# Gates and gelu rebuilt from exponentials, two projection panels swapped, in a one-core transformer kernel

## What is computed

```
lg_f = jax.nn.log_sigmoid(decay_f.astype(f32))
ret = (jax.nn.silu(rg.astype(f32)) * ret).astype(h.dtype)
```

```
h = jax.nn.gelu(blocks @ w1[j] + b1[j])
gate = jax.nn.sigmoid(gate_logits.astype(jnp.float32)).reshape(B, S, G, HPG, NSA_N_BRANCH)
```

## Time and profile before

| | us |
|---|---|
| median of 3 runs | 2376.28 |
| lowest, highest | 2376.14, 2379.73 |
| the profiled execution's own time | 2385.43 |
| its span in the profile | 2384.1 |
| ACT_TABLE_LOAD, each | 1.283 |

### The profile page before, as it was taken

One profiled execution on the slowest core, in us unless ns is written; L12 is line 12 of the kernel. 1 busy time (PEld: TensorE's weight loads), 2 busy tenths in 40 slices (PEclk: granted clock), 3 DMA queues, 4 the chain that ended last, 5 costly groups with the idle time before them and its releaser, 6 DMA issues.

```text
span 2384.1 us, 28303 instructions
## 1 busy us (share of the span) xinstructions
PE 2247.6 (94%) x11771; PEld 1653.6 (69%) x11771; DVE 1029.0 (43%) x1878; ACT 712.0 (30%) x1233; POOL 96.4 (4%) x100
## 2 busy tenths in 40 slices
PE   7999799888989989899989999999999999999998
PEld 6866588773433333378766788888878777888887
DVE  5337464441322323343557554243442455433335
ACT  4324344410100000132456333123133462331330
POOL 2100001001000000000000000000000000000001
PEclk9989899988999999999989999999999999999999
DMA  5232232268999999742110233232142201332320
GB/s 196 92 122 80 93 134 96 73 232 340 427 426 428 426 427 427 334 139 73 36 71 1 89 106 103 92 100 95 53 155 81 79 2 54 107 106 89 106 89 35
DMA packets 106740, 370.26 MB, mean 155 GB/s; under 512 B 15169, under 2 KB 20673, under 8 KB 94321
## 3 DMA queue, kind: packets, MB, share of 16 engines
q1 hardware_dynamic: 103584, 361.58, 40.1%
q0 software_dynamic: 3024, 6.83, 0.9%
HBM read 368.32 MB, written 4.19 MB: 156 GB/s over the span
## 4 chain that ended last, share of the span: by engine, by line
PE 81%; DMA 10%; DVE 5%; ACT 2%; issue 1%; POOL 0%; SPq 0%; DVEq 0%; ACTq 0%; POOLq 0%
PE PB L455 55%; PE PB L1909 9%; PE PB L472 5%; PE PB L774 4%; PE PB L465 3%; DMA Z<-in_w_exp_gate 3%; PE PB L666 3%; DMA FH_raw<-in_w_exp_gate 1%; DMA FL_raw<-in_w_exp_gate 1%; DMA Z<-in_w_exp_down 1%; DMA W_raw<-in_w_exp_down 1%; PE PB L790 1%; DMA FL_raw<-in_w_exp_down 1%; PE PB L671 1%; DVE W L447 1%
## 5 line engine op out<-in xcount | busy, mean ns | idle before, releaser
L455 PE MATMUL PB<-W,FH 128*128 128x512 f32 (+1 forms) x1792 | 556.0, 392 | 10.6 <-DVE FL L835 6.7
L447 DVE TENSOR_TENSOR W<-R,W 128x2048 fp32r<-128x2048 f32 (+1 forms) x128 | 291.3, 2276 | 609.6 <-ACT W L439 609.6
L439 ACT ACTIVATE W<-R 128x2048 fp32r<-128x2048 f32 (+1 forms) x128 | 243.4, 1902 | 646.8 <-PE PB L455 639.7
L455 PEld LDWEIGHTS PB<-W,FH 128*128 128x128 f32 x1792 | 330.9, 189 | 79.5 <-DVE FL L835 8.0
L455 PE MATMUL PB<-W,hid 128*128 128x512 f32 x1536 | 349.4, 389 | 0.0
L455 PE MATMUL PB<-W,FL 128*128 128x512 f32 (+1 forms) x896 | 347.8, 388 | 0.0
L455 PE MATMUL PB<-FH,W 128*128 128x512 f32 (+1 forms) x1152 | 325.7, 367 | 4.5 <-DVE FL L560 4.5
L455 PEld LDWEIGHTS PB<-W,hid 128*128 128x128 f32 x1536 | 288.1, 188 | 59.8
L455 PEld LDWEIGHTS PB<-FH,W 128*128 128x128 f32 x1152 | 209.6, 190 | 40.6 <-issue 5.0
L455 PE MATMUL PB<-FL,W 128*128 128x512 f32 (+1 forms) x576 | 211.2, 367 | 0.0
L455 PEld LDWEIGHTS PB<-W,FL 128*128 128x128 f32 x896 | 169.1, 189 | 34.7
(11 more groups left out here) (335 smaller groups left out, 2587.5 us busy)
## 6 DMA issues: line engine op xcount, KB each, us to landing
R<-in_mlp_w_up SPq DMA_DIRECT2D x32, 1024.0 KB, 5.2
R<-in_mlp_w_down SPq DMA_DIRECT2D x32, 1024.0 KB, 4.9
Z<-in_w_exp_down SPq DMA_DIRECT2D x14, 2048.0 KB, 29.4
Z<-in_w_exp_up SPq DMA_DIRECT2D x13, 2048.0 KB, 35.2
R<-in_w_exp_gate SPq DMA_DIRECT2D x11, 2048.0 KB, 32.3
W_raw<-in_w_exp_up SPq DMA_DIRECT2D x10, 2048.0 KB, 31.6
R<-in_w_exp_up SPq DMA_DIRECT2D x9, 2048.0 KB, 30.8
R<-in_w_in SPq DMA_DIRECT2D x12, 1024.0 KB, 5.4
```

The costliest lines, as they stand in the source:

```text
L439: k.A.e.activation(w.splits[w.split_of[u]][0][:, 0:m], w.rows(u), ACT.Copy).then_inc(*w.hi.tick(u))
L447: k.V.e.tensor_tensor(wl[:, 0:m], w.rows(u), wh[:, 0:m].bitcast(F32), ALU.subtract).then_inc(*w.lo.tick(u))
L455: ins = te.matmul(bank, l, r, start=(start and n == 0), stop=(stop and n == len(terms) - 1), skip_group_check=True)
```

## The change

In the mixer the panels of `rv` and `rg` change places: the units are swapped in the list, the Silu is applied to panel 4, DVE scales panel 5, and the decays' logarithms move from the head of panel 2 to the head of panel 5, on DVE and on ACT. In the even layer the sigmoid becomes `1 / (1 + exp(-x))`: ACT's part is an Exp, DVE adds one and takes the reciprocal of all 96 gates per partition ahead of the attention. The gelu becomes `x / (1 + exp(-2 * sqrt(2/pi) * (x + 0.044715 x^3)))`: DVE makes the argument with three operations more, ACT takes Exp one part earlier (score for weigh), and DVE adds one, takes the reciprocal and multiplies in the weigh part.

```diff
     panels("w_in", a["w_in"][0, :, 0:3072])
+    units[8:12] = units[10:12] + units[8:10]
...
-    return lambda i: (k.panel_v if p in (2, 4) else k.panel_a).at("mix", p, i)
+    return lambda i: (k.panel_v if p in (2, 5) else k.panel_a).at("mix", p, i)
...
-        if p == 2:
+        if p == 5:
             act_decay(k)
...
-            elif p == 5:
+            elif p == 4:
                 A.wait_ge(*k.projected.at("w_in", p, i))
                 ae.activation(k.rg[:, i, :], bank[:], ACT.Silu, scale=k.rstat["mix", i]).then_inc(
-                    *k.panel_a.tick("mix", 5, i))
+                    *k.panel_a.tick("mix", 4, i))
...
-        if p == 2:
+        if p == 5:
             dve_decay(k)
...
-        elif p in (2, 4):
+        elif p in (2, 5):
...
+        elif p == 4:
+            for i in range(NT):
+                V.wait_ge(*k.rqk_turned.at(i))
...
-        T.wait_ge(*k.panel_v.at("mix", 4, 3))
+        T.wait_ge(*k.panel_v.at("mix", 5, 3))
...
-        V.wait_ge(*k.panel_a.at("mix", 5, 3))
+        V.wait_ge(*k.panel_a.at("mix", 4, 3))
...
+    k.hscr = w1[:, 1408:1664]
...
-                T.wait_ge(*k.act_step.at("gelu"))
+                T.wait_ge(*k.dve_step.at("gelu"))
...
-                ae.activation(k.gates[:, i, :], bank[:, 256:280], ACT.Sigmoid).then_inc(*k.gates_out.tick(i))
+                ae.activation(k.gates[:, i, :], bank[:, 256:280], ACT.Exp, scale=-1.0).then_inc(*k.gates_out.tick(i))
...
-            elif kind == "biased" and what == "weigh":
+            elif kind == "biased" and what == "score":
                 A.wait_ge(*k.dve_step.at("biased"))
-                ae.activation(k.hrow, k.hrow, ACT.Gelu_apprx_tanh).then_inc(*k.act_step.tick("gelu"))
+                ae.activation(k.hscr, k.hscr, ACT.Exp, scale=-2.0 * math.sqrt(2.0 / math.pi)).then_inc(*k.act_step.tick("gelu"))
...
+def dve_hidden_biased(k):
+
+
+    V, ve, x, u = k.V, k.V.e, k.hrow, k.hscr
+    V.wait_ge(*k.pe_step.at("windows", 3))
+    V.settle(ve.tensor_tensor(x, k.banks["hidden",][:, 0:256], k.b1, ALU.add))
+    V.settle(ve.scalar_tensor_tensor(out=u, in0=x, scalar=0.044715, in1=x, op0=ALU.mult, op1=ALU.mult))
+    V.settle(ve.scalar_tensor_tensor(out=u, in0=u, scalar=1.0, in1=x, op0=ALU.add, op1=ALU.mult))
+    ve.tensor_scalar(u, u, -50.0, None, ALU.max).then_inc(*k.dve_step.tick("biased"))
+
+
+def dve_hidden_gelu(k):
+
+    V, ve, u = k.V, k.V.e, k.hscr
+    V.wait_ge(*k.act_step.at("gelu"))
+    V.settle(ve.tensor_scalar(u, u, 1.0, None, ALU.add))
+    V.settle(ve.reciprocal(u, u))
+    ve.tensor_tensor(k.hrow, k.hrow, u, ALU.mult).then_inc(*k.dve_step.tick("gelu"))
...
 def dve_even_attention(k):
     V, ve = k.V, k.V.e
+    V.wait_ge(*k.gates_out.at(3))
+    V.settle(ve.tensor_scalar(k.gates, k.gates, 1.0, None, ALU.add))
+    V.settle(ve.reciprocal(k.gates, k.gates))
...
             elif kind == "biased" and what == "score":
-                V.wait_ge(*k.pe_step.at("windows", 3))
-                ve.tensor_tensor(k.hrow, k.banks["hidden",][:, 0:256], k.b1, ALU.add).then_inc(*k.dve_step.tick("biased"))
+                dve_hidden_biased(k)
+            elif kind == "biased" and what == "weigh":
+                dve_hidden_gelu(k)
```

More of the change, by code:

```diff
@@ L1012, in dve_mix @@
                     *k.panel_v.tick("mix", p, i))
[L1013 to L1019, removed]
+        elif p == 4:
+            for i in range(NT):
+                V.wait_ge(*k.rqk_turned.at(i))
+                b2 = k.banks["rqk", i]
+                ve.tensor_copy(k.rqT[:, :, 128 * i:128 * i + 128], b2[:, 0:256].rearrange("p (k t) -> p k t", k=2))
+                ve.tensor_scalar(k.rkT[:, :, 128 * i:128 * i + 128],
+                                 b2[:, 256:512].rearrange("p (k t) -> p k t", k=2), 0.125, None,
+                                 ALU.mult).then_inc(*k.rk_out.tick(i))
         if p < 5:
```

## The result

The changed kernel takes 2373.14 us (median of 20 runs, 2367.63 to 2378.11) against 2379.77 for the kernel before (20 runs, the three of the first table among them, 2373.12 to 2384.12): a ratio of 0.9972 with an interval of [0.9964, 0.9980]. That is 6.6 us or 0.28% faster, just over the 4.75 us that the prediction took as its bound. 2373.14 lies inside the predicted range; the forecast "within 0.2%" missed, and "faster by over 0.2%" had been given 0.07. The profiled executions lie 16.9 us apart, far more than the medians, so the first question is which part of the 16.9 belongs to the change.

A forecast was written before the change was run, and what follows sets the result against it. PE, busy 94% of the span, was taken to bound the kernel. Mixer 0.0, gates -0.99 and gelu +0.64 gave -0.35 us against the profiled 2385.43; with the median 9.15 lower, the forecast was 2375.9, range 2372.5 to 2379.5.

The forecast's parts named there:

- within 0.2%: Whole kernel: the time changes by less than 4.75 us, what a measurement can tell from no change; chance 0.86.
- faster by over 0.2%: Whole kernel: a gain over 0.2%, needing both slow stretches to go or something unseen; chance 0.07.
- the mixer's part: Mixer: swapped panels and moved decays change nothing, 0.0 us with 0.1 either way; at most 0.10 hangs on Exp's load.
- The sign that the prediction named for the mixer: Mixer: an equal time from the last product to the first weights applied.
- the clock comes back: Even layer's first scores: with the gates' wait gone they may run fast, 1.3 us more, 2374.6; chance 0.16.
- Four loads stay four: Mixer's table loads: start, Exp, Ln, Exp in place of start, Ln, Silu, Exp.
- Gates, -0.99: Even layer's gates: without the sigmoid's table load PE gains its whole wait, 0.99 us.
- Gelu, +0.64: Even layer's gelu: PE starts the hidden values' turn at 1209.86 against 1209.22, a loss of 0.64 us.
- the second chain: DVE's later gelu steps: start at 1207.41, cost 0.23 plus a 256-column reciprocal of 1.55 plus 0.43 us.
- PE's apply part: Near the gelu: begins 1.4 us late, takes 1.13, ends at 1208.4 ahead of 1209.22, so costs nothing by itself.
- The slow clock lasts longer: Behind the gelu: more PE idle time keeps the clock down, giving 2383 us; chance 0.05.
- The change does not do what it says: Gates: something else takes over PE's wait at 1154.65, only the gelu's loss stays, 2376.9 us; chance 0.06.

The follow-up runs named there:

- 3: Changed kernel plus one unread 8-column Exp behind the decays' Ln, so the Exp table loads early: 2377.56 us, ratio 0.9998 to the kernel before.
- 4: Kernel before plus one redundant wait on ACT ahead of the mixer attention's first Exp, so its table loads late: 2374.36 us, ratio 0.9985.
- 5: Kernel before plus 16 spare transposes in PE's wait ahead of the mixer's first apply part: 2373.19 us, ratio 0.9979.
- 11: Kernel before plus 16 spare transposes in the mixer's wait and the gates' sigmoid as an Exp: 2371.93 us, ratio 0.9973.
- 1: Kernel before plus the mixer's part of the change alone: 2374.52 us, ratio 0.9990.
- 9: Kernel before with the panels swapped, the decays left in panel 2 and the even layer as before: 2375.29 us, ratio 0.9990.
- 8: Kernel before with the decays' logarithms at the head of panel 5, panels not swapped: 2377.41 us, ratio 0.9997.
- experiment 12: The changed kernel run once more, unedited: 2370.23 us, ratio 0.9973 to the kernel before.

## Why the prediction was right or wrong

**The failed step** is in the mixer's part. Of the load for the first Exp it said "0.10 us at most hangs on it" and "so even the 0.10 is swallowed", and of the whole part "I count 0.0 us, with 0.1 either way". It took the load's place for given and only asked what its removal could give. But the swap takes the Silu away from the end of panel 5, ACT then has two waits ahead of its first Exp, and the load gets behind both. By the prediction's own way of counting this is a loss of 1.25 us (PE's wait of 2.33 for 1.08) that the DMA's 6.85 us swallow. They do swallow it; what I missed is that the moved pause of PE sets the clock of the 16 us that follow. Experiments 3 and 4 show the load's part of this both ways. That the pause is the link rests on the one profile and the median of 5, and on the median of 11 (7.2 us under before, of which 1 was expected of the gates) against its profile; it is likely, and less surely shown than the load's part. In the marks it is worth 5 to 7 us. In the medians of 1, 4 and 9 it is about 4, and each of these intervals, some 3 us either way, just reaches no change; it is the marks, in two groups without overlap, that carry the verdict.

The sign that the prediction named for the mixer, an equal time from the last product to the first weights applied, came true (9.06 us from the first scores to the first weights before, 9.03 after) and could not have caught this: the time is lost behind it.

**The range held by luck.** It was laid around 2376.28, the median of three runs. The kernel before came to 2379.77 over twenty; laid around that, the same range would be 2376.0 to 2383.0, and 2373.14 would be outside. The sum had -0.35 us, and -6.6 were measured.

**The list of unknowns.** The prediction read the granted clock for the even layer alone, and priced "the clock comes back" there alone. The mixer's 16 us at 0.50 could be read in the same view, and are longer than any stretch it looked at.

**Loads.** "Four loads stay four" was wrong: five, since the Silu of panel 4 needs its own and its neighbours changed. The total is 9, not 8 (12 before). The two at L1062 and L1064 delay nothing: I found no wait of PE there.

**Gates, -0.99.** Right in place and size. From the turn before the wait to the one behind it PE takes 3.40 us before and 2.40 after. PE's timeline, before (the turn behind the wait is in the earlier trace rows) and after:

```profile
1151.25 0.60 PE L472 MATMUL PB<-ident,nsp 128*128 128x128 f32 x4
```

```profile
1138.75 0.60 PE L473 MATMUL PB<-ident,nsp 128*128 128x128 f32 x4
...
1141.15 0.66 PE L473 MATMUL PB<-ident,nsp 128*128 128x128 f32 x4
```

The reciprocal of 96 columns took 0.75, the upper end of 0.62 to 0.75; it had ended 0.23 us before the extremum could start.

**The first rival, "the clock comes back", came true** at the even layer's scores, with its 1.3 us. In the seven profiles with the gates as an Exp these eight matmuls took 1.99 each time. In the seven with the sigmoid they took 3.29 to 3.54 in four and 1.99 in three (4, 8, 9). So the low clock came there in four of seven profiles with the wait and in none of seven without it; I gave that 0.16. It does not make the layer faster by 1.0 and 1.3: the averages of the stretch from the layer's head to the odd layer's load differ by 1.2 in all.

**Gelu, +0.64.** At the turn of the hidden values the sign and the mechanism were right, and the size was 1.0. That this passes on to the end, as the sum took it to, is not shown: at the odd layer's load the kernels with and without it do not differ (741.17 and 741.18 us from the layer's head, on average, with the gates as an Exp). Three terms were a little under: the one-input form took 0.29 for 0.23, the reciprocal 1.75 (the upper bound) for 1.55, and the second chain began 2.59 us behind the bias for 2.44. The slope from 4 to 256 columns is (1752 - 178) / 252 = 6.2 ns a column:

```profile
L2678 DVE RECIPROCAL W_raw<-W_raw 128x256 f32<-128x256 f32 x1 | 1.8, 1752 | 0.0
...
L2786 DVE RECIPROCAL Z<-Z 128x96 f32<-128x96 f32 x1 | 0.8, 754 | 0.0
```

One more step was off: PE's apply part took 1.92 us and not 1.13: PE had waited 2.81 us ahead of it, and the granted clock is 0.50 from 1193.66 to 1199.66. It ended at 1195.50, still before the hidden values came at 1195.79.

**The other rivals.** "The slow clock lasts longer" did not come. (Its own sum comes to 2384.0 and not to 2383: 2376.28 - 0.99 + 7.4 + 1.3.) Over the 32 us around the gelu that hold the same 125 rows of PE the granted clock is 0.68 before and 0.73 after:

```profile
1204.00:1236.00 32.00, 24.80 (x125) 19.36 (x123) 16.48 (x69) 16.26 (x59) 2.54 (x4) 0.68 0.24 92
```

```profile
1190.00:1222.00 32.00, 24.10 (x125) 18.18 (x124) 20.98 (x80) 14.56 (x60) 2.53 (x4) 0.73 0.24 89
```

"The change does not do what it says" is out by the gates. The sum by the traces is: mixer -5 to -7, and the even layer about -1.2 in all, as an average of profiles that lie up to 4 us apart; measured -6.6 (interval -4.8 to -8.6).

**Open:** why the fillings kept the clock in 5 and not in 11, and what decides at the even layer's scores with the sigmoid, and where in the even layer the gelu's 1.0 us is made up. No run here separates these.

## What to carry to other kernels

Before costing an edit at nothing, look at the granted clock behind every pause of PE that the edit can move, not only at what ends the wait: a pause that is hidden behind a DMA can still halve the speed of the work after it. Where an activation function changes place, count the waits ahead of its successor as well, since the compiler's table load went in front of one wait and behind two; here that is a lever of its own, worth about 4 us by the median with one redundant wait. And try the cheap half of such a change by itself: with ACT's own gelu and the rest as changed the kernel took 2370.35 us, and its ratio of 0.9962 [0.9946, 0.9978] is the lowest measured, though its lead over the changed kernel (0.9972 and 0.9973) is inside the intervals, and the traces show no such lead in the even layer.

## What the runs showed of the hardware

- The place of PE's pause counts, not its length alone: between 156 and 168 us PE idled 4.3 us before and 3.7 after, but over 164 to 180 us the granted clock was 0.50 in the kernel before, with PE busy without a break from 168 on, and 1.00 in the changed one. In experiments 1 and 4 PE idled 5.2 us between 156 and 168, more than before, and the clock stayed at 1.00 all the while. Place and length do not settle it either: the pauses of experiments 5 and 11 were nearly the same, and the clock fell in 11 alone.
- Eight matmuls of 64x512 took 7.19 us at the low level and 3.70 at the high one; the eight of the first scores 3.54 and 1.99.
- The same kernel's runs lie 11.6 us apart (experiment 12, 2367.61 to 2379.21), and one stretch of 825 us without any edit scatters by 8. The Trainium skill ("TensorE: Matmul & The Clock Gate", Part 1, on the clock gate) says that the activity monitor runs free of the kernel, so that one kernel's count of slow matmuls at its start differs from run to run. The spread here, in the middle of a kernel, would fit that, but no run here shows that this is its cause; and the mixer's slow stretch came in every profile with the early load but one of the two filled ones.
- A reciprocal takes 178 ns for 4 columns, 754 for 96 and 1752 for 256; a table load 1.28 us, with the next activation 0.01 us behind it.
